# A hybrid encoder block on one core: four hand-overs between stages are reordered

## The reference

```python
h = rmsnorm(x, norm1_g)
p = h @ w_in                      # u, v, c_q, c_kv, k_rope, gate_A, gate_B
a = chunked_gmlp(gelu(u), gelu(v)) @ w_a_out       # y = u * (W_s v + b), 128-token chunks
b = latent_attention(c_q, c_kv, k_rope) @ w_b_out  # 8 heads, softmax over all tokens
x = x + (sigmoid(gate_A) * a + sigmoid(gate_B) * b) @ w_out
t = rmsnorm(x, norm2_g)
aff = softmax(t @ w_router)       # 16 experts; each takes its 128 (prompt) and 32 (sample) best tokens
x = x + sum over experts of gate * (silu(t @ w_gate) * (t @ w_up)) @ w_down
```

## Time and profile before

| | |
|---|---|
| time, three runs | 2048.7, 2052.22, 2052.87 us, median 2052.22 |
| the profiled execution | 2048.8 us, its span 2047.0 |
| TensorE busy | 2017.8 us, 99% |
| VectorE, ScalarE, GpSimd busy | 66%, 47%, 46% |
| mean granted TensorE clock | 0.998 |

### The profile page before, as it was taken

One profiled execution on the slowest core, in us unless ns is written; L12 is line 12 of the kernel. 1 busy time (PEld: TensorE's weight loads), 2 busy tenths in 40 slices (PEclk: granted clock), 3 DMA queues, 4 the chain that ended last, 5 costly groups with the idle time before them and its releaser, 6 DMA issues.

```text
span 2047.0 us, 33422 instructions
## 1 busy us (share of the span) xinstructions
PE 2017.8 (99%) x13208; PEld 1674.3 (82%) x13208; DVE 1346.9 (66%) x1600; ACT 966.2 (47%) x1205; POOL 940.6 (46%) x665
## 2 busy tenths in 40 slices
PE   8999999999999999999999999999999999999997
PEld 8888888888889889889988888777777777777775
DVE  7865455456777477777754378676776677676674
ACT  7212211113555376666641133466665556656663
POOL 0985555566655376666643636412232222222221
PEclk9999999999999999999999999999999999999999
DMA  4323544333677622132134564878877888888873
GB/s 155 106 106 135 168 161 141 130 93 122 231 249 258 224 65 88 65 106 83 47 117 163 171 202 165 306 315 312 300 273 283 302 314 314 313 315 309 291 272 109
DMA packets 180586, 403.17 MB, mean 197 GB/s; under 512 B 16896, under 2 KB 99840, under 8 KB 180480
## 3 DMA queue, kind: packets, MB, share of 16 engines
q1 hardware_dynamic: 165744, 348.63, 46.5%
q0 software_dynamic: 7680, 20.98, 4.5%
q10 hardware_dynamic: 7056, 32.12, 4.4%
HBM read 322.38 MB, written 79.30 MB: 196 GB/s over the span
## 4 chain that ended last, share of the span: by engine, by line
PE 87%; DVE 5%; ACT 2%; DMA 2%; issue 1%; POOL 1%; SPq 0%; ACTq 0%; DVEq 0%; POOLq 0%
PE PS L1917 24%; PE PS L480 13%; PE PS L481 13%; PE PS L482 13%; PE PS L1965 8%; PE PS L1670 3%; PE PS L1653 1%; PE PS L1657 1%; PE PS L1654 1%; PE PS L1655 1%; PE PS L1656 1%; PE PS L1593 1%; PE PS L1476 1%; PE PS L1901 1%; PE PS L2046 1%
## 5 line engine op out<-in xcount | busy, mean ns | idle before, releaser
L480 PE MATMUL PS<-act_hi,w_hi 128*128 128x256 f32 (+1 forms) x800 | 275.1, 344 | 1.5 <-issue 0.7
L481 PE MATMUL PS<-act_lo,w_hi 128*128 128x256 f32 (+1 forms) x800 | 270.1, 338 | 0.0
L482 PE MATMUL PS<-act_hi,w_lo 128*128 128x256 f32 (+1 forms) x800 | 269.7, 337 | 0.0
L1176 POOL TENSOR_SCALAR prob<-prob,small 128x1024 f32<-128x1024 f32 x64 | 185.6, 2901 | 109.9 <-DVE small L2920 109.9
L1279 POOL DMA_INDIRECT y_s<-ob_s,ixs_s x16 | 44.2, 2762 | 350.0 <-DVE ob_s L3215 350.0
L3119 DVE TENSOR_TENSOR elo<-raw,ehi 128x2048 fp32r<-128x2048 f32 x63 | 144.2, 2290 | 35.1 <-ACT ehi L2555 35.1
L480 PEld LDWEIGHTS PS<-act_hi,w_hi 128*128 128x128 f32 x800 | 151.8, 190 | 18.1 <-issue 1.9
L482 PEld LDWEIGHTS PS<-act_hi,w_lo 128*128 128x128 f32 x800 | 151.5, 189 | 16.3
L481 PEld LDWEIGHTS PS<-act_lo,w_hi 128*128 128x128 f32 x800 | 151.9, 190 | 14.6 <-issue 0.7
L1917 PE MATMUL PS<-ehi,xT_hi 128*128 128x512 f32 x492 | 155.1, 397 | 1.5 <-DVE elo L3119 1.5
L1917 PE MATMUL PS<-elo,xT_hi 128*128 128x512 f32 x492 | 152.0, 390 | 0.0
(11 more groups left out here) (421 smaller groups left out, 5541.9 us busy)
## 6 DMA issues: line engine op xcount, KB each, us to landing
raw<-in_w_gate SPq DMA_DIRECT2D x63, 1024.0 KB, 7.9
raw_w<-in_w_up SPq DMA_DIRECT2D x32, 1024.0 KB, 16.4
raw_more<-in_w_up SPq DMA_DIRECT2D x30, 1024.0 KB, 13.1
w_raw<-in_w_in SPq DMA_DIRECT2D x16, 1024.0 KB, 7.7
w_raw<-in_w_down SPq DMA_DIRECT2D x15, 1024.0 KB, 6.2
stg<-in_w_down SPq DMA_DIRECT2D x15, 1024.0 KB, 7.9
gt<-in_w_down SPq DMA_DIRECT2D x15, 1024.0 KB, 9.9
raw_end<-in_w_down SPq DMA_DIRECT2D x15, 1024.0 KB, 14.3
```

The costliest lines, as they stand in the source:

```text
L480: pe.matmul(out, lh, rh, start=first, stop=False)
L481: pe.matmul(out, lh, rl, start=False, stop=False)
L482: return pe.matmul(out, ll, rh, start=False, stop=last)
L1176: pool.tensor_scalar(prob[:, n % 3], prob[:, n % 3], prec[:, c:c + 1], None, ALU.mult).then_inc(S["norm_pool"], 1)
```

## The change

- SyncE: g1b is issued behind row 1 of x, not behind row 0.
- GpSimd rounds the first two weight tiles in place of ScalarE. ScalarE copies rows 0 and 1 rounded first and raw after, row 1 before row 0, row 0 behind VectorE's subtraction; VectorE takes row 0 from PSUM. The second weight tile's subtraction stands behind two more scalings. Fillers: 40 and 4 in place of 28 and 9.
- VectorE: y_part 1 and 2 stand behind the sums and the latent steps. TensorE's waits there are as they were.
- ScalarE computes one exponential of one element ahead of the attention.
- The second half of b_row(0, 1) stands behind values(68); ScalarE's o_part(3) stands behind high(70).
- residual(7, 1) stands two picks earlier.

```diff
 def high_no(c):
-    return 2 * c + 1 if c < NCH_P else 2 * NCH_P + 1 + c - NCH_P
+    return c + 1 if c < 2 else 2 * c + 1 if c < NCH_P else 2 * NCH_P + 1 + c - NCH_P
 def raw_no(c):
-    return 2 * c + 2
+    return 4 - c if c < 2 else 2 * c + 2
@@ SyncE
-                if n == 0:
+                if n == 1:
                     sp.dma_start(g1b[:], ...)
@@ GpSimd
+            for j in range(2):
+                pool.wait_ge(w_in_s[j], 16)
+                pool.tensor_scalar(w_hi[:, j], w_raw[:, j], 1.0, 0.0, ALU.mult, ALU.add).then_inc(S["w_rounded"], 1)
@@ TensorE
-            keep_on(28)
+            keep_on(40)
             n1_turn(0)
-            keep_on(9)
+            keep_on(4)
...
-            def b_row(j, k):
+            def b_row(j, k, halves=(0, 1)):
...
-                for b in range(2):
+                for b in halves:
...
                 if n == STEPS:
-                    for k in range(2):
-                        b_row(0, k)
+                    b_row(0, 0)
+                    b_row(0, 1, (0,))
                 if 2 <= n < STEPS + 2:
                     turn_prob(n - 2)
                 if n >= 4:
                     values(n - 4)
+                if n == STEPS:
+                    b_row(0, 1, (1,))
@@ ScalarE
-                if n < NCH_P:
-                    act.activation(h_raw[:, :, n * P:(n + 1) * P], src, ACT.Copy).then_inc(S["n1_hi"], 1)
-            def first_high(j):
-                act.wait_ge(w_in_s[j], 16)
-                act.activation(w_hi[:, j], w_raw[:, j], ACT.Copy).then_inc(S["w_rounded"], 1)
+                if 1 < n < NCH_P:
+                    n1_raw(n)
+            def n1_raw(n):
+                if n == 0:
+                    act.wait_ge(S["n1_lo"], 1)
+                src = bank(4 if n % 2 else 6, D).rearrange("p (k t) -> p k t", k=KD)
+                act.activation(h_raw[:, :, n * P:(n + 1) * P], src, ACT.Copy).then_inc(S["n1_hi"], 1)
             n1_high(0)
-            first_high(0)
             n1_high(1)
-            first_high(1)
+            n1_raw(1)
+            n1_raw(0)
...
+            act.activation(exp_warm, epsc, ACT.Exp)
             for n in range(STEPS + 4):
...
+                if n == STEPS:
+                    o_part(3)
...
-                if returns_at(n) is not None:
+                if returns_at(n) is not None and n != STEPS - 1:
                     o_part(returns_at(n))
@@ VectorE
             def n1_low(n):
-                if n < NCH_P:
+                if n == 0:
+                    dve.wait_ge(S["n1_hi"], high_no(0))
+                    src = bank(6, D).rearrange("p (k t) -> p k t", k=KD)
+                elif n < NCH_P:
...
             n1_low(1)
-            first_low(1)
             n1_scale(2)
             n1_scale(3)
+            first_low(1)
...
-            for k in range(3):
-                y_part(k)
+            y_part(0)
             for n in range(4, 7):
                 total(P_LAST, n)
             dve.wait_ge(S["latent_act"], 11)
...
-            y_part(3)
-            y_part(4)
+            for k in range(1, 5):
+                y_part(k)
...
-            select(0, 39, 45)
+            select(0, 39, 43)
             residual(7, 1)
-            select(0, 45, PICKS)
+            select(0, 43, PICKS)
```

## The result

The changed kernel takes 2054.44 us (median of 20 runs, 2052.47 to 2059.64), the one before 2051.45 us (20 runs, 2048.5 to 2054.96). The ratio is 1.0019, with an interval from 1.0013 to 1.0025: 3.9 us slower (2.7 to 5.1). The forecast was slower by 5.0 us. The profiled execution took 2055.05 us (span 2052.0); the one of before had a span of 2047.0, so the profiles are 5.0 us apart.

The account below looks back on a forecast made before the run. The prediction took TensorE, busy 99% of the span, as the bound; its terms, -0.2 + 4.9 + 2.7 - 0.8 - 0.2 - 1.4 = +5.0 us, on the 2052.22 median gave 2057.2 us, range 2050.5 to 2061.0.

Parts of the forecast that it names:

- Part 2: Seam before the attention's projections: both 0.87 us stands go, TensorE stands 7.8 us on late y_part(1); +4.9 us.
- the lower branch: Seam: VectorE's ckv_lo goes before GpSimd's 0.6 us operation, so y_part(1) ends at 525.6 instead of 527.3.
- The clock's term: Behind the new seam stand: clock falls, 5.5 us of products run at half pace; +2.7 us, bounds 0 and 2.7.
- Parts 3, 4 and 5: First softmax's table load hidden, -0.8 us; last softmax's transposes earlier, -0.2; router's 1.47 us stand nearly gone, -1.4.
- Part 1: Start of the kernel: later rows come 0.2 us earlier, GpSimd's roundings hidden; -0.2 us, between -1.0 and +1.0.
- The sum: Whole kernel: all parts and the clock together give +5.0 us, 2057.2 us on the median.
- (b): Rival at the seam: the stand comes but the clock holds; +2.3 us, 2054.5 us; chance 0.22.
- (c): Rival at the seam: no turns, y_part(1) ends at 523.3, clock holds; -0.8 us, 2051.4 us; chance 0.12.
- (d): Rival at the start: freed ScalarE brings every row sooner; -4 us there and (c) elsewhere, 2047.5 us; chance 0.05.
- (e): Rival at the start: the moved filler collides and costs 1.0 us more; 2058.4 us; chance 0.03.

Follow-up runs that it names:

- the run without turns: The changed kernel with GpSimd's splits of the projection weights held until y_part(1) is done; ratio 1.0016 to the kernel before.
- the order alone: The kernel before with only the new order of y's low parts; 2056.07 us, ratio 1.0028.
- the four edits: Projections-a-row-later kernel with y_part(3) behind the first cq_lo, query weights' split behind the second, and 13 second-seam fillers; 2044.67 us, ratio 0.9966.
- the run with all but the order: The changed kernel with y's low parts in the order of before; 2048.9 us, ratio 0.9989.
- the one with y_part(2) between: The changed kernel with y_part(1) ahead of the sums and y_part(2) between sums and latents; ratio 0.9989.
- the start alone: The kernel before with the new start only; one execution, second row's transposes 0.34 us later, +0.22 us carried on.

## Why the prediction held, step by step

**Part 2, and the forecast with it, was right in its mechanism.** TensorE stood on y_part(1), both 0.87 stands went, and so did the two behind the seam. That this order is the whole loss is shown from both sides, by putting it back and by making it alone. Expected +4.9, measured +3.5: +6.1 from 515 to 535.6, less the clock's 2.6. The term was too large by the choice of the middle between 525.6 and 527.3 for y_part(1)'s end. VectorE was first, by 0.03 us, so the lower branch held, and at 525.0 it was still 0.6 us quicker than worked out, 0.2 of which is the earlier start of ckv_lo. A race decided by so little should have been carried as two cases, not as a mean that can't happen.

**The clock's term** was 2.7, measured 2.60 in the trace and 2.59 by taking it away. That the clock would fall was right, and the size was luck. The half pace lasted 5.5 us as at the start of the kernel, but in the run without turns it lasted 3.1 and cost 1.45, in the order alone 3.9 and 1.8. The two rows that the term was built on vary as much: in the thirteen profiles the full clock came 3.8 to 6.1 us after the first filler (5.5 before), and after the kernel's last product it was granted for another 2.1 to 5.1 us (2.9 before). In the stand itself it fell 5.1 us after the last product, in the order alone 3.5, without turns 4.5.

The Trainium skill, "TensorE: Matmul & The Clock Gate", Part 1, warns against idle gaps in the middle of a kernel; the traces with the new order agree, 1.00 to 0.50 at 523.7 with TensorE idle from 518.6. The turns agree with the Trainium skill, "SBUF — State Buffer", section "SBUF: two separate sides", by which the engine that comes second to the shared port pair waits until the first is done: with GpSimd kept out, two cq_lo took 3.14 us, with it 4.25.

**Parts 3, 4 and 5:** -0.88, -0.19 and -1.45 in the profile, where -0.8, -0.2 and -1.4 were forecast, the first and the last confirmed alone. **Part 1:** -0.25 forecast as -0.2, but within the landing's scatter. GpSimd's rounding of a weight tile, put at 1.2 us, took 1.77; it stayed hidden.

**The sum** was +5.0 and the profiles are 5.1 apart at the last product. That is closer than its terms: the seam was 1.4 too dear, and 1.8 us of longer stands at 604, 748 to 920, 1195 and 1335 were in no term. The prediction said that between stands nothing waits on anything not itself paced by TensorE, and that was wrong: TensorE waits for a head's queries to land (748), and at 1335 for experts' weights that are split when they have landed. Such stands come and go between executions: from 712 to 1000 it is +0.5 here, between -0.2 and +2.2 in ten other profiles and +4.1 in the eleventh, most of them above zero, since the profiled execution of before was one of the quick ones. The ratio of many runs, +3.9, is about what the measured parts give without them (3.5 + 2.6 - 0.25 - 0.88 - 0.19 - 1.45 = 3.3). Of the rivals, (b) failed at the clock, (c) at the clock and at the end of y_part(1), 525.0 against the 524 from which it would decide, (d) and (e) at a start that moved by 0.25 us. That (b)'s 2054.5 is nearest to the measured time is chance: the kernel before has a median of 2051.45 over 20 runs, and 1.0019 times the 2052.22 from which the forecast started is 2056.1, 1.1 us under it.

Some of the prediction's sums do not come out. With y_part(1) at 527.3 its own steps give 527.4 + 4.86 - 526.10 - 0.4 = +5.8 and not +6.1 for part 2. Rival (e) costs 1.0 more than 2057.2, which is 2058.2 and not 2058.4. The ends of the range are not what their words give either: (c) with a quick run is some 3.4 under 2051.4, about 2048, and +6.1 for part 2 with the clock is 2058.4, so that 2050.5 to 2061.0 is about 2.5 us too high at both ends. The measured 2054.44 lies in either.

## What to carry to other kernels

Before moving a piece of work behind others on one engine, look up by its number when the consumer asks for that piece: the gain of earlier sums was 2 us, the price of a late y_part(1) a stand of 6.6 us and the clock. Where two engines work in turns and both are full, another order may only move the waits (0.9989 with two orders of the same work); what won here (0.9966) was to give TensorE other work meanwhile, to ask for each part when its producer has it, and to keep GpSimd's work that nobody needs yet out of the stretch (and 13 fillers in the second seam; the four edits were not measured apart). If a stand of several us can't be avoided, fill it: 50 small transposes gave back 2.6 us here.

## What the runs showed of the hardware

A fall of the clock in mid-kernel does not take five us of stand, and a longer stand doesn't always bring it. In the seam at 1335 and at a head's load, with code that no edit here touched, the granted clock fell behind stands of 2.2 to 2.5 us in four profiled executions (1.3 us lost by 1345 in each of the three at the first of these places), and once more behind the 2.3 us before the first projection. At 1335 it held in two others, over stands of 2.4 and 3.4 us:

```profile
1338.00:1340.00 2.00, 2.00 (x6) 0.50 1.02 416
```

```profile
1336.07 0.73 PE L1922 MATMUL PS<-ehi,xT_hi 128*128 128x512 f32 x2 [3.20 <-DVE elo L3133]
...
1336.00:1340.00 4.00, 3.94 (x18) 1.00 1.03 421
```

```profile
1336.92 0.73 PE L1920 MATMUL PS<-ehi,xT_hi 128*128 128x512 f32 x2 [2.20 <-DVE elo L3127]
...
1336.90:1341.00 4.10, 4.08 (x19) 1.00 1.04 420
```

The first fence is of the run with all but the order, the second of the one with y_part(2) between, the third of the start alone. What decides is open: of the seven mid-kernel stands of 2.2 to 3.4 us in the thirteen profiles five were followed by a fall and two were not, and behind the shorter ones, up to 1.9 us, none came. It may be a part of why executions of one kernel lie 4 to 8 us apart; no run here shows that.
